# Gate, value and projection panels of two fused transformer blocks summed by token, with the gated sums turned by TensorE ahead of the output projections

## The reference

```python
# first block
mod = silu(c) @ w_ada + b_ada                       # six vectors of 2048: shifts, scales, gates
h = rms_norm(x, g) * (1 + sc1) + sh1
u, q, k, v, ga, gb = split(h @ w_in)                # 1024, 1024, 1024, 1024, 2048, 2048 columns
y_ssm = s5_branch(u, ...)                           # state-space scan, gelu, then y * sigmoid(y @ w_glu + b_glu)
y_att = attention(q, k, v, rel_bias)                # 8 heads of 128
merged = sigmoid(ga) * (y_ssm @ w_proj_ssm) + sigmoid(gb) * (y_att @ w_proj_attn)
x = x + g1 * (merged @ w_out)
x = x + g2 * (square(relu(h2 @ w_ff1)) @ w_ff2)     # 2048 -> 8192 -> 2048
# second block, on rms_norm of that x
xr, yr, q, k, v, g_rnn, g_attn = split(h @ w_in)
y_rnn = rg_lru(conv(xr)) * gelu(yr); y_att = window_attention(q, k, v, sinks)     # 32 query heads of 64
mix = sigmoid(g_rnn) * (y_rnn @ w_rnn_proj) + sigmoid(g_attn) * (y_att @ w_attn_proj)
x = x + rmsnorm(mix @ w_out)
x = x + rmsnorm(square(relu(h @ w_mlp_up)) @ w_mlp_down)
```

## Time and profile before

| | |
|---|---|
| time, median of 3 runs | 3098.48 us (3096.87 to 3098.67) |
| span of the profiled execution, first to last instruction | 3094.2 us |
| median less span | 4.3 us |
| mean granted TensorE clock | 0.985 of full |
| instructions | 48738 |
| TensorE matmul, busy | 2996.5 us (97%) |
| VectorE, busy | 2056.6 us (66%) |
| ScalarE, busy | 1389.9 us (45%) |
| GpSimd, busy | 246.1 us (8%) |
| HBM read | 624.66 MB, 203 GB/s over the span |

### The profile page before, as it was taken

How to read it: one execution, slowest core, us unless ns; L and a number is a source line. 1 busy time by engine, 2 the same in 40 slices (tenths; PEclk the granted TensorE clock), 3 DMA queues, 4 the chain that set the end, 5 groups by cost and what they waited for, 6 DMA issues and landing times.

```text
span 3094.2 us, 48738 instructions
## 1 busy us (share of the span) xinstructions
PE 2996.5 (97%) x20315; PEld 2724.7 (88%) x20315; DVE 2056.6 (66%) x2372; ACT 1389.9 (45%) x1704; POOL 246.1 (8%) x253
## 2 busy tenths in 40 slices
...
GB/s 328 318 194 191 187 238 288 264 298 279 184 263 242 258 196 188 194 189 158 178 164 165 182 181 152 150 148 178 190 184 176 187 185 185 197 186 195 187 193 153
DMA packets 303513, 632.06 MB, mean 204 GB/s; under 512 B 21856, under 2 KB 26352, under 8 KB 302720
## 3 DMA queue, kind: packets, MB, share of 16 engines
...
HBM read 624.66 MB, written 4.21 MB: 203 GB/s over the span
## 4 chain that ended last, share of the span: by engine, by line
PE 88%; DVE 6%; DMA 3%; ACT 2%; issue 1%; SPq 0%; ACTq 0%; DVEq 0%
PE PS L1006 19%; PE PS L993 12%; PE PS L995 12%; PE PS L994 12%; PE PS L1010 10%; PE PS L1022 7%; PE PS L1024 7%; PE PS L1023 7%; DVE wlo L1933 1%; DMA F<-in_w_ada 1%; DMA raw<-in_w_in 1%; ACT whi L2468 1%; DMA raw<-in_w_ada 1%; DVE aacc L1922 1%; DVE F L1666 1%
## 5 line engine op out<-in xcount | busy, mean ns | idle before, releaser
L1933 DVE TENSOR_TENSOR wlo<-raw,whi 128x1024 fp32r<-128x1024 f32 x867 | 1083.5, 1255 | 770.6 <-ACT whi L2468 769.7
L2468 ACT ACTIVATE whi<-raw 128x1024 fp32r<-128x1024 f32 x867 | 914.4, 1059 | 1145.6 <-PE PS L995 410.4
L993 PE MATMUL PS<-R,whi 128*128 128x256 f32 x3584 | 1033.2, 288 | 27.1 <-DVE wlo L1933 20.0
L994 PE MATMUL PS<-R,whi 128*128 128x256 f32 x3584 | 1020.3, 285 | 0.0
L995 PE MATMUL PS<-R,wlo 128*128 128x256 f32 x3584 | 1020.1, 285 | 0.0
L993 PEld LDWEIGHTS PS<-R,whi 128*128 128x128 f32 x3584 | 694.0, 194 | 43.1 <-DVE wlo L1933 24.3
L994 PEld LDWEIGHTS PS<-R,whi 128*128 128x128 f32 x3584 | 694.6, 194 | 0.6 <-issue 0.5
L995 PEld LDWEIGHTS PS<-R,wlo 128*128 128x128 f32 x3584 | 694.0, 194 | 0.0
L1006 PE MATMUL PS<-R,whi 128*128 128x512 f32 x2496 | 628.7, 394 | 10.8 <-DVE R L1843 5.4
L1006 PEld LDWEIGHTS PS<-R,whi 128*128 128x128 f32 x2496 | 451.8, 190 | 92.8 <-issue 11.5
L1010 PEld LDWEIGHTS PS<-R,wlo 128*128 128x128 f32 x2496 | 341.9, 191 | 24.5
...
...
## 6 DMA issues: line engine op xcount, KB each, us to landing
...
raw<-in_w_mlp_up SPq DMA_DIRECT2D x128, 512.0 KB, 3.9
raw<-in_w_mlp_down SPq DMA_DIRECT2D x128, 512.0 KB, 4.0
...
```

The source lines that it names most:

```text
L993: pe.matmul(o, whi[:, s, c:c + P], x.operand.hi(k), start=first, stop=False, skip_group_check=True)
L994: pe.matmul(o, whi[:, s, c:c + P], x.operand.lo(k), start=False, stop=False, skip_group_check=True)
L1933: v.tensor_tensor(wlo[:, i % SPN, :], words(j), whi[:, i % SPN, :].bitcast(F32), ALU.subtract).then_inc(lo_done, 1)
L2468: a.activation(whi[:, i % SPN, :], words(j), ACT.Copy).then_inc(hi_done, 1)
```

## The change

Panels part 2 to 4, ga, gb, v, ps, pa, gr, rp, gt and ap are summed by token; of two sums only ff1 is left. The gates and both branches' projections then lie with tokens on partitions, so that gating and adding go on as before on tiles of the same size (`gate2` now serves ap too, and the steps that added two sums are gone). The v panels come out as attention wants them, and one ScalarE copy each (`values`) takes the place of copy, transposes and second copies. The merged sum has to have features on partitions for w_out and wo2, so TensorE turns it: `turn_merged`, 8 transposes for each of the panels pa 0 to 3 and ap 0 to 3, two ticks after the panel's last unit, into banks 4 to 7; `gate_hi` and the lo part read PSUM, three ticks after the panel's last unit where it was one. The extra pair of raw slots now lies at V for all units from 104 to 440. Line numbers here are those of the file before (minus) and after (plus).

```diff
...
         self.by_token = by_token
 
-        self.two_sums = name in ("ff1", "ap") or name == "gt" and i > 0
+        self.two_sums = name == "ff1"
         self.banks = 4 if self.two_sums else 2
         self.ids = list(range(first, first + units))
 
...
@@ -384,23 +383,23 @@
     by_h, by_h_b = (lambda k: (h_ready, k + 1)), (lambda k: (h_ready, k + 9))
 
     for i in range(5):
-        panel("part", i, w_in, 0, 8, i * 512 if i < 2 else 4096 + (i - 2) * 512, h, by_h, a_once.at("part%d" % i))
+        panel("part", i, w_in, 0, 8, i * 512 if i < 2 else 4096 + (i - 2) * 512, h, by_h, a_once.at("part%d" % i), i > 1)
     for i in range(2):
         panel("u", i, w_in, 8, 8, i * 512, h_b, by_h_b, (evac_v["u"], i + 1))
     for i in range(3):
-        panel("ga", i, w_in, 8, 8, 4096 + i * 512, h_b, by_h_b, v_once.at("ga%d" % i))
-    panel("ga", 3, w_in, 0, 16, 4096 + 1536, h, by_h, (evac_a["ga"], 4))
+        panel("ga", i, w_in, 8, 8, 4096 + i * 512, h_b, by_h_b, v_once.at("ga%d" % i), True)
+    panel("ga", 3, w_in, 0, 16, 4096 + 1536, h, by_h, (evac_a["ga"], 4), True)
     for i in range(4):
-        panel("gb", i, w_in, 0, 16, 6144 + i * 512, h, by_h, (evac_a["gb"], i + 1))
+        panel("gb", i, w_in, 0, 16, 6144 + i * 512, h, by_h, (evac_a["gb"], i + 1), True)
     for i in range(2):
         for name, c0 in (("q", 1024), ("k", 2048), ("v", 3072)):
-            panel(name, i, w_in, 0, 16, c0 + i * 512, h, by_h, (evac_a[name], i + 1))
+            panel(name, i, w_in, 0, 16, c0 + i * 512, h, by_h, (evac_a[name], i + 1), name == "v")
     for i in range(2):
         panel("glu", i, w2("w_glu"), 0, 8, i * 512, yg, lambda k: (yg_ready, k + 1), (ys_ready, i + 1))
     for i in range(4):
-        panel("ps", i, w2("w_proj_ssm"), 0, 8, i * 512, ys, lambda k: (ys_ready, k // 4 + 1), (evac_v["ps"], i + 1))
+        panel("ps", i, w2("w_proj_ssm"), 0, 8, i * 512, ys, lambda k: (ys_ready, k // 4 + 1), (evac_v["ps"], i + 1), True)
     for i in range(4):
-        panel("pa", i, w2("w_proj_attn"), 0, 8, i * 512, ya, lambda k: (ya_ready, k + 1), (evac_v["pa"], i + 1))
+        panel("pa", i, w2("w_proj_attn"), 0, 8, i * 512, ya, lambda k: (ya_ready, k + 1), (evac_v["pa"], i + 1), True)
     for i in range(4):
         panel("w_out", i, w2("w_out"), 0, 16, i * 512, mg, lambda k: (mg_ready, k // 4 + 1), (evac_v["res1"], i + 1))
...
@@ -426,13 +425,13 @@
         panel("yr", i, w_in2, 0, 16, 2048 + i * 512, H, by_H, (yr_a, 3 * i + 1))
     panel("KV", 0, w_in2, 0, 16, 6144, H, by_H, (q_a, 6))
     for i in range(4):
-        panel("gr", i, w_in2, 0, 16, 6656 + i * 512, H, by_H, (evac_a["gr"], i + 1))
+        panel("gr", i, w_in2, 0, 16, 6656 + i * 512, H, by_H, (evac_a["gr"], i + 1), True)
     for i in range(4):
-        panel("rp", i, w2("w_rnn_proj_2"), 0, 16, i * 512, xc, lambda k: (yr_ready, k // 4 + 1), (evac_v["rp"], i + 1))
+        panel("rp", i, w2("w_rnn_proj_2"), 0, 16, i * 512, xc, lambda k: (yr_ready, k // 4 + 1), (evac_v["rp"], i + 1), True)
     for i in range(4):
-        panel("gt", i, w_in2, 0, 16, 8704 + i * 512, H, by_H, (evac_v["gt"], i) if i else (evac_a["gt"], 1))
+        panel("gt", i, w_in2, 0, 16, 8704 + i * 512, H, by_H, (evac_a["gt"], i + 1), True)
     for i in range(4):
-        panel("ap", i, w2("w_attn_proj_2"), 0, 16, i * 512, YA, lambda k: (YA_ready, k // 4 + 1), (evac_v["ap_sum"], i + 1))
+        panel("ap", i, w2("w_attn_proj_2"), 0, 16, i * 512, YA, lambda k: (YA_ready, k // 4 + 1), (evac_v["ap"], i + 1), True)
     for i in range(4):
         panel("wo2", i, w2("w_out_2"), 0, 16, i * 512, MG, lambda k: (mg_ready, 4 + k // 4 + 1), (evac_a["wo"], i + 1))
...
@@ -537,8 +536,7 @@
     pair = lambda i, a, b: {i: fv(a, 1024), i + 1: fv(b, 1024)}
     tables, outputs = pair(RAWN, E0, E0 + 1024), pair(RAWN + 2, CT, CT + 1024)
     more = ((0, NXN, tables, None), (NXN, NWIDE, {**tables, **outputs}, (x_copied, 8)), (NWIDE, NSTART, outputs, (x_copied, 8)),
-            (at_unit[104], at_unit[117], pair(RAWN, K + 1024, V + 1024), (y_done, 16)),
-            (at_unit[137], at_unit[440], pair(RAWN, V, V + 1024), (v_turned, 4)))
+            (at_unit[104], at_unit[440], pair(RAWN, V, V + 1024), (y_done, 16)))
 
     def time_of(j):
         return next((t for t in more if t[0] <= j < t[1]), None)
@@ -816,15 +814,22 @@
                 free[4 + i % 2] = (bh_copied, i + 1)
                 yield
 
-        def turn_v(g):
-            pe.wait_ge(evac_a["v"], g + 1)
-            for i in range(2):
-                wait_bank(7)
-                for hd in range(4 * g, 4 * g + 4):
-                    t = pe.transpose(PS[:, 7, (hd % 4) * P:(hd % 4) * P + P], v3[:, hd, i * P:i * P + P], ident[:, :])
-                t.then_inc(v_turned, 1)
-                free[7] = (v_copied, 2 * g + i + 1)
-                yield
+        def turn_merged(i, off, n0):
+
+            g = f3(off + 1024 * i, 2, 512)
+            yield
+            yield
+            pe.wait_ge(mg_sum, n0 + i + 1)
+            for b in range(2):
+                bank = 4 + 2 * (i % 2) + b
+                wait_bank(bank)
+                for m in (2 * b, 2 * b + 1):
+                    for j in range(2):
+                        o = (m % 2) * T + j * P
+                        t = pe.transpose(PS[:, bank, o:o + P], g[:, j, m * P:m * P + P], ident[:, :])
+                free[bank] = (mg_ready, n0 + i + 1)
+            t.then_inc(mg_turned, 1)
+            yield
 
         def head(hd):
...
@@ -843,7 +848,7 @@
             yield
             vh = slice(hd * P, hd * P + P)
             pe.wait_ge(pt_copied, hd + 1)
-            pe.wait_ge(v_copied, 2 * (hd // 4) + 2)
+            pe.wait_ge(evac_a["v"], hd // 4 + 1)
             pe.matmul(PS[:, ba, 0:256], vn[:, 0, vh], pt[:, 0:256], start=True, stop=False, skip_group_check=True)
             pe.matmul(PS[:, ba, 128:256], vn[:, 1, vh], pt[:, 256:384], start=False, stop=True,
                       skip_group_check=True).then_inc(av_done, 1)
...
@@ -1051,10 +1056,8 @@
                 new.append(row_close(ROW_CLOSE.index(n)))
             if n == end_of["k", 0] + 2:
                 new.append(bias_tiles())
-            for i in range(2):
-                if n == end_of["v", i] + 2:
-                    new.append(turn_v(i))
             new += [head(hd) for hd in range(8) if n == HEAD_TICK[hd]]
+            new += [turn_merged(*m) for m in merges(n)]
             if n == end_of["w_out", 3]:
                 stats_by_tile("stat2", SQ_RES1 + 3, 0, a_once.at("std2"))
             if n == end_of["ff1", 15] + 3:
@@ -1080,6 +1083,16 @@
     HEAD_TICK = [end_of["v", 0] + 2] * 3 + [end_of["v", 0] + 10] + [end_of["v", 1] + 2] * 3 + [end_of["v", 1] + 11]
     PAIR_TICK = [end_of["KV", 0] + 1 + 4 * (pr % 2) + 8 * (pr // 2) for pr in range(16)]
     SOFTPLUS_TICK = end_of["ff1", 4]
+
+    def merges(n):
+
+        x = ends.get(n)
+        return [(x.i, *TURNED[x.name])] if x is not None and x.name in TURNED else []
+
+    def turned_bank(i):
+        return PS[:, 4 + 2 * (i % 2):6 + 2 * (i % 2), :].rearrange("p a n -> p (a n)")
+
+    TURNED = {"pa": (GB, 0), "ap": (GT, 4)}
     MERGE_TICK = [end_of["rp", 3] + t for t in (1, 2, 3, 5)]
 
...
@@ -1457,32 +1470,15 @@
         def gate2(x, off, off1, done, made, op, n0):
             g = fv(off + 1024 * x.i, 1024)
             v.wait_ge(*passed(x.name, x.i))
+            v.wait_ge(evac_a["gb" if x.name == "pa" else "gt"], x.i + 1)
             v.wait_ge(made, 4)
             v.scalar_tensor_tensor(g, g, 1.0, banks(x), ALU.add, ALU.mult).then_inc(done, 1)
             v.wait_ge(done, x.i + 1)
             v.tensor_tensor(g, g, fv(off1 + 1024 * x.i, 1024), ALU.add).then_inc(mg_sum, 1)
-            yield
+            for e in range(3):
+                yield
             v.wait_ge(mg_hi, n0 + x.i + 1)
-            v.scalar_tensor_tensor(op.lo(4 * x.i, 4), g, 0.5, op.hi(4 * x.i, 4).bitcast(F32), ALU.mult, ALU.subtract).then_inc(mg_ready, 1)
-
-        def gate_sum(x):
-            v.wait_ge(evac_a["gt_low"], x.i)
-            two_added(x, fv(GT + 1024 * x.i, 1024), evac_v["gt"])
-            yield
-
-        def gate3(x):
-            g, t_ = fv(GT + 1024 * x.i, 1024), ap_low(x.i)
-            v.wait_ge(evac_a["ap_low"], x.i + 1)
-            two_added(x, t_, evac_v["ap_sum"])
-            v.wait_ge(evac_v["ap_sum"], x.i + 1)
-            v.wait_ge(evac_a["gt"], 4)
-            v.scalar_tensor_tensor(g, g, 1.0, t_, ALU.add, ALU.mult).then_inc(evac_v["ap"], 1)
-            v.wait_ge(evac_v["ap"], x.i + 1)
-            v.wait_ge(evac_v["rp"], 4)
-            v.tensor_tensor(g, g, fv(1024 * x.i, 1024), ALU.add).then_inc(mg_sum, 1)
-            yield
-            v.wait_ge(mg_hi, 4 + x.i + 1)
-            v.scalar_tensor_tensor(MG.lo(4 * x.i, 4), g, 0.5, MG.hi(4 * x.i, 4).bitcast(F32), ALU.mult, ALU.subtract).then_inc(mg_ready, 1)
```

(43 more changed lines are left out.)

29 lines of the change are left out of this document (12 added, 17 removed).

## The result

| | before | after |
|---|---|---|
| time, median | 3097.68 us (3096.09 to 3098.67, 4 runs) | 3060.86 us (3058.68 to 3061.57, 4 runs) |
| ratio to before | | 0.9885, 95% interval 0.9872 to 0.9899 |
| span of the profiled execution | 3094.2 us | 3060.3 us |

The kernel is 36.8 us faster by the medians (31 to 40 by the interval) and 33.9 us by the profiled spans; forecast were 31.5 us and 3067 us, range 3055 to 3079. A second set of runs of the changed kernel, further down, gave 3061.07 us and a span of 3059.7, 32.3 us under the median of the kernel before on the same chip (3093.40).

The account below looks back on a forecast made before the run. TensorE, busy 97% of the span, was taken to bound the kernel except where stages wait for something else. Terms 25.7 + 4.1 - 4.8 + 0.5 + 6.0 = 31.5 us, from 3098.5 to 3067 us; range 3055 to 3079.

Parts of the forecast that it names:

- Form of the sums: Panels changed to by-token sums: 25.7 us saved against by feature (17.9 to 29.4), plus 4.1 us against two sums.
- The rule of 2.5 ns a matmul: In all changed panels: fixed issue gap makes the form worth some 6 us, not 30; as rival 3092 us, chance 0.02.
- Transposes: Eight added turns in pa and ap cost 7.0 us, removed turns of v save 1.7; net cost 4.8 us.
- The merge: Gate and sum before the turns in pa and ap: ready about when TensorE comes, no wait counted; gain 0.5 us.
- Rival (e): At the eight turns: sums late, TensorE held and clock falls; 3.9 us each eats the gain, 5 gives 3107; chance 0.04.
- The slots: glu 1 and ps 0: six slots, not four, from unit 117 to 137 relieve the stall; gain 6.0 us, ends 0 and 13.2.
- Rival (d): At the eight turns: transposes lower the clock, losing 14 to 27 us, about 3087 us; chance 0.03.

## Why the prediction was right

The direction, the size and the place of most of the gain came out: 31.5 us forecast, 33.9 us of span and 36.8 us of median measured. That the total is so near is in part luck: the form gave 2 us less than forecast, and the slots and w_out 1 gave 1.6 and 1.9 us more. By its steps:

- **Form of the sums.** Panels of gt 1 to 3 and ap 0 fell by 0.59 us, exactly as taken from the earlier trace rows. In gb, ga 3 and ga 2 the saving is 1.19 for 8 units (0.60 for 4), in gr and rp 1.04, not 1.28. The missing part is at the side pieces, and I took it as nothing ("each tick gets 0.16 us shorter around it"). The second matmul after a piece is late in both forms: by 0.11 us by token (below, 0.34 us instead of 0.23), by 0.10 by feature (0.22 instead of 0.12). The form differs behind it: by token the next five to ten matmuls come 0.23 to 0.24 us apart, where 0.227 is the rule, and by feature they do not. A gr panel has four pieces; what they cost altogether is 27.38 - 21.76 = 5.62 us by token and 28.41 - 23.04 = 5.37 by feature, 0.06 us a piece. In gb there are two. The sum of this term was 25.7 and is 23.7 by the table (5.9 + 1.2 + 2.2 + 8.2 + 1.2 + 1.8 + 0.6 for ps + 2.6 for pa). Putting either block back gave the same prices again.
- **The rule of 2.5 ns a matmul** (the Trainium skill, "TensorE: Matmul & The Clock Gate", section "Back-to-back issue gap") does not describe this stream. The page gives it for an isolated matmul and says itself that weight loads between the matmuls change it, which my prediction left out. By it the second block's 16 panels by feature would cost 16 x 96 x 2.5 ns = 3.8 us, about what its turns give back (3.6), and they cost 14.8 after the turns.
- **Transposes.** Forecast 0.87 us for eight, measured 0.85 to 0.94. Some 7.2 us were added (7.0 forecast) and 1.7 removed.
- **The merge.** No wait at any of the eight turns, as forecast, and the margin was rightly read as thin: one tick less costs 2 us in pa and next to nothing in ap; two ticks less cost 33 us of span. Rival (e) is a real mechanism, clock included: 4.4 us a turn measured, 3.9 put. Two `yield` lines are what keeps it away. ScalarE's wait for the sum went as forecast (before, below), and with it pa's own idle: pa 2 takes 12.41 us before and 11.52 with the first block put back by feature, 0.9 us where I had counted 0.5.
- **The slots.** The step was right, its size too small. 6.0 us were forecast for the stall in glu 1 and ps 0, 7.6 came (8.2 less the form's 0.6), and putting the slots back cost 9.3, with more low clock than before. I had kept 2 us of the softmax wait and most of the low clock. Its mechanism was half seen: the late transfer was late also by the jump of the numbering at unit 137, which the change took away with the switch, and I did not look at it.
- **What I did not count.** w_out 1 fell by 2.3 us to its own 23.04: it no longer waits (1.8 us in two waits before); I had credited 0.4 us for it. None of the parts put back brings this back: w_out 1 takes 23.04 to 23.09 us in every later kernel. What all of them have in common against before is that ScalarE does not stand in `gate_hi` for 23.2 us through pa, so units are converted and their slots filled again sooner; with that the transfers are at 93 to 95% of their time through ps and pa. That this is the cause fits, but it was not tried alone. Against these gains stand 3.2 us more ahead of ga 1. With the one trace of before it can't be told whether that is the change's: eleven later traces with the same parts reach ga 1 between 210.8 and 215.4 us; before reached it at 211.0.
- **Rival (d).** The clock is 1.00 in the windows with turns, once and doubled. It falls where TensorE waits ahead of a turn, not where it turns.

ScalarE's wait for the sum in `gate_hi`, before, from 641 to 700 us:

```profile
ACT R L2212 <- DVE F L1463: 23.2, 4, 7.6
```

The piece that ends in a pair's step, in the changed kernel and then before:

```profile
1923.39 0.39 PE L898 MATMUL PS<-F 64*128 64x128 f32 x4
1923.70 0.50 PE L1027 MATMUL PS<-whi,R 128*128 128x512 f32 x1
1924.04 0.39 PE L1028 MATMUL PS<-whi,R 128*128 128x512 f32 x1
1924.27 0.40 PE L1029 MATMUL PS<-wlo,R 128*128 128x512 f32 x1
```

```profile
1894.66 0.39 PE L993 MATMUL PS<-R,whi 128*128 128x256 f32 x1
1894.88 0.28 PE L994 MATMUL PS<-R,whi 128*128 128x256 f32 x1
```

The 3 us by which the median's gain exceeds the span's are scatter. In every run listed with both, before and after, the time is 1.3 to 1.4 us above the same run's span. The 4.3 us that I took for what lies around the span were that and the luck of the profiled execution: with a span of 3094.2 it took some 3095.5 us, under the median of 3097.7, while 34 further runs of the kernel before lie between 3091.0 and 3100.6. The forecast did not suffer, as it set out from the median.
